# Small matmuls of three head groups, issued bank by bank instead of alternating between two banks

## What is computed

```python
# A: sliding-window attention, 8 heads of 64, 2 key heads, chunks of 64
logits = einsum('bcqhgd,bckhd->bchgqk', qc, kb) * 64**-0.5 + bias
# B: retention, 4 heads, keys of 64, values of 128
scores = einsum('bclhd,bcshd->bchls', qc, kc) * decay_in
y = einsum('bchls,bcshe->bclhe', scores, vc) + einsum('bclhd,bchde->bclhe', qc, R_prev) * q_decay
# C: Mamba-2 SSD, 8 heads of 64, state of 64, 2 groups
y_diag = einsum('bclsgj,bcsgjp->bclgjp', CB[..., None] * Lmat, xdt)
y_off = einsum('bclgn,bcgjpn->bclgjp', Cm, h_prev) * exp(a_cum)[..., None]
y = y_diag + y_off + D * xs
```

## Time and profile before

| what | value |
| --- | --- |
| median of three executions | 1348.97 us (1345.64 to 1350.3) |
| the profiled execution's own time | 1350.3 us |
| its span, first to last instruction | 1348.5 us |
| mean granted TensorE clock | 0.992 of full speed |
| TensorE (PE) matmul busy | 1307.2 us, 97% |
| VectorE (DVE) busy | 656.3 us, 49% |
| ScalarE (ACT) busy | 626.8 us, 46% |
| GpSimd (POOL) busy | 575.6 us, 43% |

### The profile page before, as it was taken

How to read it: one execution, slowest core, us unless ns; L and a number is a source line. 1 busy time by engine, 2 the same in 40 slices (tenths; PEclk the granted TensorE clock), 3 DMA queues, 4 the chain that set the end, 5 groups by cost and what they waited for, 6 DMA issues and landing times.

```text
span 1348.5 us, 21792 instructions
## 1 busy us (share of the span) xinstructions
PE 1307.2 (97%) x6226; PEld 1052.8 (78%) x6226; DVE 656.3 (49%) x935; ACT 626.8 (46%) x965; POOL 575.6 (43%) x433
## 2 busy tenths in 40 slices
PE   6999999999999999999999999999999999999995
PEld 4787777777888888888877878777778888888884
DVE  6856557456444203443267556664744431144423
ACT  6432376266666423334363224835576652233433
POOL 3533334153544544544444334242544444444443
PEclk8999999999999999999999999999999999999998
DMA  6322222132333333333322222121323333333333
GB/s 194 92 70 70 58 69 79 48 86 71 113 98 100 99 97 86 93 94 101 102 73 86 79 63 75 51 71 55 110 78 94 101 100 104 100 93 93 94 99 104
DMA packets 65656, 119.47 MB, mean 89 GB/s; under 512 B 7320, under 2 KB 8632, under 8 KB 65464
## 3 DMA queue, kind: packets, MB, share of 16 engines
q1 hardware_dynamic: 65592, 118.64, 31.0%
HBM read 116.12 MB, written 2.49 MB: 88 GB/s over the span
## 4 chain that ended last, share of the span: by engine, by line
PE 82%; DVE 10%; issue 4%; ACT 3%; DVEq 0%; DMA 0%; ACTq 0%; SPq 0%
PE dense L894 73%; PE mix L894 7%; DVE arena L647 2%; DVE h_lo L572 2%; DVE ssq L578 1%; ACT w_hi L382 1%; PE mix L1076 1%; DVE arena L669 0%; DVE arena L840 0%; DVE arena L842 0%; DVE pad L637 0%; DVE arena L644 0%; DVE arena L885 0%; PE mix L993 0%; DVE x L628 0%
## 5 line engine op out<-in xcount | busy, mean ns | idle before, releaser
L323 POOL TENSOR_TENSOR w_lo<-w_raw,w_hi 128x512 fp32r<-128x512 f32 x428 | 575.2, 1361 | 762.7 <-ACT w_hi L382 747.8
L894 PE MATMUL dense<-h_hi,w_hi 128*128 128x512 f32 x1152 | 458.8, 398 | 16.2 <-ACT w_hi L369 6.4
L894 PE MATMUL dense<-h_lo,w_hi 128*128 128x512 f32 x1152 | 450.9, 391 | 0.0
L382 ACT ACTIVATE w_hi<-w_raw 128x512 fp32r<-128x512 f32 x424 | 249.3, 622 | 183.3 <-PE dense L894 181.0
L894 PE MATMUL dense<-h_hi,w_lo 128*128 128x512 f32 x1152 | 310.2, 391 | 0.0
L894 PEld LDWEIGHTS dense<-h_hi,w_hi 128*128 128x128 f32 x1152 | 217.7, 189 | 69.1 <-issue 15.4
L894 PEld LDWEIGHTS dense<-h_lo,w_hi 128*128 128x128 f32 x1152 | 217.9, 189 | 46.9 <-issue 2.7
L894 PEld LDWEIGHTS dense<-h_hi,w_lo 128*128 128x128 f32 x1152 | 217.8, 189 | 45.9
L894 PE MATMUL dense<-m_hi,w_hi 128*128 128x512 f32 x544 | 217.3, 400 | 3.2 <-ACT w_hi L382 2.5
L894 PE MATMUL dense<-m_lo,w_hi 128*128 128x512 f32 x544 | 211.9, 390 | 0.0
L894 PE MATMUL dense<-m_hi,w_lo 128*128 128x512 f32 x544 | 146.8, 389 | 0.0
(11 more groups left out here) (165 smaller groups left out, 1051.8 us busy)
## 6 DMA issues: line engine op xcount, KB each, us to landing
w_raw<-in_w SPq DMA_DIRECT2D x428, 256.0 KB, 2.7
x<-in_xT SPq DMA_DIRECT2D x8, 256.0 KB, 5.1
out_y<-arena SPq DMA_DIRECT2D x8, 256.0 KB, 2.1
consts<-in_consts SPq DMA_DIRECT2D x1, 1283.0 KB
rel_scratch<-arena SPq DMA_DIRECT2D x1, 382.0 KB
bias<-rel_scratch SPq DMA_DIRECT2D x8, 32.0 KB, 2.1
params<-in_params SPq DMA_DIRECT2D x1, 154.5 KB, 2.3
wdt_raw<-in_wdt SPq DMA_DIRECT2D x1, 64.0 KB
```

The lines of the kernel that those rows point to most:

```text
L323: nc.gpsimd.tensor_tensor(w_lo[:, s, :], w_raw[:, s, :], w_hi[:, s, :].bitcast(f32), ALU.subtract).then_inc(lo_ready, 1)
L382: nc.scalar.activation(w_hi[:, slot, :], w_raw[:, slot, :], ACT.Copy).then_inc(hi_ready, 1)
L894: return T.matmul(dst, lhsT, rhs, start=start, stop=stop)
```

## The change

In AS, RA, SB and RB the matmuls are issued in another order. No matmul is added or taken away, and no operand changes. In AS and RA the loop over the banks (g or j) becomes the outer one: all matmuls of one bank, and then all of the other. In SB and RB each inner (diag) matmul is followed at once by the cross matmul into the same place, and the banks follow one another. The flags of the accumulation follow the new order. Each bank is handed over behind its own last matmul, and waited for (take) ahead of its own first one. In RB the wait for the state of the block before stands ahead of the first matmul of a bank. In blocks 0 of SB and RB, which have no cross matmuls, the order stays.

```diff
                         for g in range(2):
+                            r = slice(64 * g, 64 * g + 64)
                             take(name, 1 + g, l)
                             for jj in range(4):
                                 h, tt, hh = 4 * g + jj, jj // 2, jj % 2
                                 d = M[4 + g][64 * hh:64 * hh + 64, P * tt:P * tt + P]
-                                ins = mm(d, xdt[:, 64 * h:64 * h + 64], lm[:, g, jj, :], tt == 0, n == 0 and tt == 1)
-                            if n == 0:
-                                ins.then_inc(m_ready[4 + g], 1)
-                        if n:
-                            for jj in range(4):
-                                tt, hh = jj // 2, jj % 2
-                                for g in range(2):
-                                    r = slice(64 * g, 64 * g + 64)
-                                    d = M[4 + g][64 * hh:64 * hh + 64, P * tt:P * tt + P]
-                                    ins = mm(d, hst[r, n % 2, 64 * jj:64 * jj + 64], cs[r, jj, :], False, tt == 1)
-                                    if jj == 3:
-                                        ins.then_inc(m_ready[4 + g], 1)
+                                ins = mm(d, xdt[:, 64 * h:64 * h + 64], lm[:, g, jj, :], True, n == 0)
+                                if n:
+                                    ins = mm(d, hst[r, n % 2, 64 * jj:64 * jj + 64], cs[r, jj, :], False, True)
+                            ins.then_inc(m_ready[4 + g], 1)
...
-                        take(name, 0, l)
-                        take(name, 1, l)
-                        for c in range(2):
-                            ch = 2 * n + c
-                            for m in range(2):
-                                at = 256 * c + P * m
-                                for g in range(2):
-                                    r = slice(64 * g, 64 * g + 64)
+                        for g in range(2):
+                            r = slice(64 * g, 64 * g + 64)
+                            take(name, g, l)
+                            for c in range(2):
+                                ch = 2 * n + c
+                                for m in range(2):
+                                    at = 256 * c + P * m
                                     ins = mm(M[g][:, at:at + P], aq[r, ch, P * m:P * m + P],
                                              ak[r, CH * ch:CH * ch + P])
-                                    if c == 1 and m == 1:
-                                        ins.then_inc(m_ready[g], 1)
+                            ins.then_inc(m_ready[g], 1)
...
-                        take(name, 1, l)
-                        take(name, 2, l)
-                        for t in range(2):
-                            for j in range(2):
-                                r = slice(64 * j, 64 * j + 64)
+                        for j in range(2):
+                            r = slice(64 * j, 64 * j + 64)
+                            take(name, 1 + j, l)
+                            for t in range(2):
                                 ins = mm(M[1 + j][:, P * t:P * t + P], rk[r, t, blk], rq[r, t, blk])
-                                if t == 1:
-                                    ins.then_inc(m_ready[1 + j], 1)
+                            ins.then_inc(m_ready[1 + j], 1)
...
                         for j in range(2):
+                            r = slice(64 * j, 64 * j + 64)
                             take(name, j, l)
+                            if n:
+                                pe.wait_ge(m_free[5], ready(f"RB{n - 1}", 2, l) + 1)
                             for t in range(2):
                                 h = 2 * t + j
-                                ins = mm(M[3 + j][:, P * t:P * t + P], vtok[:, n, h, :], rpt[:, h, :],
-                                         t == 0, n == 0 and t == 1)
-                            if n == 0:
-                                ins.then_inc(m_ready[3 + j], 1)
-                        if n:
-                            pe.wait_ge(m_free[5], ready(f"RB{n - 1}", 2, l) + 1)
-                            for t in range(2):
-                                for j in range(2):
-                                    r = slice(64 * j, 64 * j + 64)
-                                    ins = mm(M[3 + j][:, P * t:P * t + P], rst[r, t, :], qd[r, t, :], False, t == 1)
-                                    if t == 1:
-                                        ins.then_inc(m_ready[3 + j], 1)
+                                d = M[3 + j][:, P * t:P * t + P]
+                                ins = mm(d, vtok[:, n, h, :], rpt[:, h, :], True, n == 0)
+                                if n:
+                                    ins = mm(d, rst[r, t, :], qd[r, t, :], False, True)
+                            ins.then_inc(m_ready[3 + j], 1)
```

## The result

The changed kernel takes 1388.43 us (median of four executions, 1384.06 to 1390.82). The kernel before takes 1349.63 us (four, 1345.64 to 1350.85). The ratio is 1.0277, 95% interval 1.0246 to 1.0310. So the change costs 38.8 us by the medians; the ratio stands for 37.4 us, with an interval from 33.2 to 41.8. The forecast was 1384 us, 35 us more.

A forecast was written before the change was run, and what follows sets the result against it. TensorE, busy 97% of the span, was taken as the bound, so its added time shows in full. Terms 25.8 + 10.3 + 0 + 0 - 1.1 = 35.0 us gave 1385.3 on the profiled execution, hence 1384 us; range 1362 to 1398.

The forecast's parts named there:

- SB, 16 groups of 0.37: SB blocks 1 to 3, six times: alternating shapes make 16 groups of 0.37 us, 5.92 against 1.62; +25.8 us in all.
- RB, 8 groups of 0.43: RB blocks 1 to 3, six times: 8 groups of two matmuls, 3.34 us against 1.63; +10.3 us in all.
- AS, full overlap: AS, eight times: upper-half matmuls overtake and still run beside the lower half's, despite 16 instructions to pass; 0 us.
- RA, full overlap: RA, eight times: upper half passes eight instructions, as SA0 shows, and runs beside the lower half; 0 us.
- wait of RV0: RV0 behind SB3: bank 4 handed over earlier shortens TensorE's wait for VectorE by 0.55 us, -1.1 us in both layers.
- the line through pairs and quartets: SB group price from 8 pairs (1.02 us) and 4 quartets (0.60): 0.39 us, upper bound +27.7 us.
- The case of shared cells: Rival in SB: shapes wait only where they share array cells, column halves run side by side; 8.0 us, total 1366; chance 0.15.
- the two bounds that I had kept: AS, per step: 0 with full overtaking, or +0.88 us in strict order (1.97 against 1.09), 7.0 us in all.
- rival of an AS that is partly serial: AS overlaps only partly: 1385 to 1391 us; chance 0.22 together with AS, or AS and RA, serial.
- Strict order: Rival in AS and RA: matmuls start in program order; up to 10.5 us more, 1394; chance 0.22, partly serial AS included.
- The clock: Rival in SB: short groups with gaps drop the clock to half; 8 to 17 us on top, 1392 to 1401; chance 0.09.
- No cost: Rival: TensorE gathers matmuls of one shape, so the new order costs nothing; 1348 us; chance 0.04 within 0.3%.

## Why the prediction was right, and where not

| step | predicted, us in all | measured in the traces |
| --- | --- | --- |
| SB, 16 groups of 0.37 | +25.8 | 6 x (6.21 - 2.06) = +24.9 |
| RB, 8 groups of 0.43 | +10.3 | 6 x (3.81 - 2.22) = +9.5 |
| AS, full overlap | 0 | 8 x (1.64 - 1.09) = +4.4 |
| RA, full overlap | 0 | 0 |
| wait of RV0 | -1.1 | 2 x (0.70 - 1.23) = -1.1 |
| wait at AT1, behind line 792 | not seen | -1.1 |
| wait behind RV1, for line 382 | not seen | 2 x (0.81 - 1.14) = -0.7 |
| sum | +35.0 | +35.9; medians +38.8 |

*The bound.* TensorE sets the time, and what it loses in the mixed steps shows nearly in full. This held: the busy time of the other engines hardly moved, and the lengths add up to the 35.9 us of the mixed stretches. The medians' 38.8 us are 2.9 more, within the interval of the ratio, which is about 4 us to either side. Not quite in full, since TensorE's idle time in each mixed stretch also fell by 1.2 us, of which only the 0.53 at RV0 was foreseen.

*Luck.* That the sums lie only 0.9 us apart is partly luck. AS was put 4.4 us too low. Against it stand 0.9 us too much for SB, 0.8 for RB, and 1.8 us of waits that vanished unforeseen. The mechanism and the two large terms were right; the sum owes its closeness to small errors that cancel.

*SB.* A change of shape every two instructions costs 0.36 us per group. The row of two transposes in RA0, 0.36 us, was the exact price. I took 0.37, between it and the line through pairs and quartets, and so the term was 0.9 us too large. The case of shared cells fell at once: groups in different column halves wait for each other too. It agrees with what the Trainium skill states in TensorEngine Tiling (Array Packing), Key Properties, that a change of tiling mode drains TensorE. The experiment with cross on 128 partitions shows that the shape is the cause. The price has two parts, which the prediction's sum held without saying so. By 0.36 = 0.15 + 2 x 0.105, an estimate from these rows, the gaps at 14 more changes of shape make up about half of the 4.15 us. The other half, 2.1 us, are instructions that ran beside each other before, two or four at a time, and now run one by one: 32 x 0.105 against 12 x 0.105.

*RB.* The same mechanism, and 0.8 us less than predicted, because a group of two costs 0.42 and not 0.43, and the first one 0.31.

*AS.* This is the step that was mis-sized. "I take 0 for both, because the one overtaking that the trace shows had no visible limit" was wrong for AS. There is a limit, and 16 instructions lie beyond it. The measured value lies between the two bounds that I had kept, 0 and 0.88 us, at 0.55, which is 4.4 us in all. The case that came true is thus the forecast for SB and RB together with the rival of an AS that is partly serial. For RA the argument held, since SA0 showed just that number of instructions.

*Strict order* as a rival: wrong. RA would have taken 1.09 us by it, and it took 0.65. The Trainium skill states that order in TensorE: Matmul & The Clock Gate, Part 3: matmuls start in program order. The trace disagrees where the matmuls are on different halves of the array.

*The clock* as a rival: wrong. The granted clock is 1.00 over the whole mixed stretch of the changed kernel in both layers, though SB is only short groups there.

*No cost*, by gathering matmuls of one shape: wrong. In these traces TensorE passed matmuls for another part of the array, and never one of another shape.

*The waits.* RV0 went as predicted. I didn't look for waits behind AS. The one at AT1 and the one behind RV1 were filled by the longer AS.

## What to carry to other kernels

Count the changes of matmul shape (how many partitions, how many columns) in TensorE's order before counting matmuls: here each cost 0.15 to 0.21 us. Then count what runs side by side, for a matmul alone between two changes has no company in the rest of the array. The change cost 34 us in SB and RB; by the estimate above some 20 are the 120 added changes, and some 15 the lost company. Removing a few changes from the kernel before, with one wait filled, gave 0.6%. Sort small matmuls by shape first and by bank second, and alternate between array halves every matmul, or every second one (0 to 0.10 us for a step here; runs of four cost 0.55). A bank that is handed over earlier is worth something only where TensorE waits for it.

## What the runs showed that I had not expected

TensorE's overtaking has a limit. An instruction for the free half starts once no more than six instructions of the other half ahead of it haven't started. With 8 ahead that is at once (RA, 0.65 us for the step), with 12 at the third matmul (1.42 us), with 16 at the fifth (1.64 us). The single records show the upper half's first load right behind the third and the fifth matmul. So a run of matmuls for one half must be short for the other half to run beside it from the start. The rule is read from matmuls of 64 partitions by 128 columns; no run tried another shape.
